# Moving residual passes, operand splits and gate rows in the instruction streams of VectorE and ScalarE of a two-layer transformer trunk

## The chip, the cores and the metric

The kernel runs on one core of a Trainium2 chip, as one launch. The metric is the device time of a run in microseconds. Of the kernel before there are three timed runs: 1076.07, 1076.11 and 1076.93 us, median 1076.11 us. One further execution was profiled; the rows below come from it.

## The reference

A trunk of two layers works on x (256 tokens, 1024 channels, float32). From a condition vector c come nine vectors of shift, scale and gate per layer, and two more for the shared keys and values. Each layer has three sub-layers, and each ends in a residual and a LayerNorm:

```python
def post_norm_residual(x, y, gate, weight, g, b):
    return layer_norm(DEEPNORM_ALPHA * x + weight * (1.0 + gate[:, None, :]) * y, g, b)
# cond = silu(c); per layer l:
mod = (cond @ w_ada[l] + b_ada[l]).reshape(b, 9, d)
h = modulate(x, mod[:, 0], mod[:, 1])                 # x * (1 + scale) + shift
x = post_norm_residual(x, swiglu(h, w_ffn_in[l, 0], w_ffn_out[l, 0]), mod[:, 2], 0.5, ...)
h = modulate(x, mod[:, 3], mod[:, 4])
# layer 0: q, k, v from h; rotary on 32 of 128 dims of q and k; causal softmax (256 tokens are one block)
# layer 1: q from h; k, v shared, from x before the layer; stick-breaking attention
y = merge_heads(y) @ w_o[l]
x = post_norm_residual(x, y, mod[:, 5], 1.0, ...)
h = modulate(x, mod[:, 6], mod[:, 7])
x = post_norm_residual(x, swiglu(h, w_ffn_in[l, 1], w_ffn_out[l, 1]), mod[:, 8], 0.5, ...)
```

There are 8 heads of 128 dims; the FFN has 2816 inner channels, done here in 11 steps of 256.

## The kernel before, in words

Every weight matrix is read once from HBM in 164 chunks of 128 x 2048 float32 (1 MB). SyncE loads chunk n into one of five buffers `raw`. ScalarE copies it to a float32r tile, the high part (`split_hi(n)`, L504); VectorE subtracts that from the raw chunk and gives the low part (`split_lo(n)`, L837). TensorE then makes each product of three float32r matmuls: high by high, low by high, high by low (`three`, L1253 to L1255 for products of the modulated input; `add_rows`, L1328 to L1330 for products that add up the sub-layer's output). High and low tiles have five places (`SPL`); a chunk may be split only when the chunk that held its place has been used. SyncE may load chunk n when chunk n-5 has its low part.

There is no scheduler and no planner: each engine has one stream of instructions, written out by hand, and runs it strictly in that order. Engines meet through semaphores alone. So an instruction that waits holds back all that stands behind it on its engine.

The stages in order are: FFN 0 (chunks 0 to 32), norm 0, QKV projection with rotary turn and softmax attention (33 to 44), output projection (45 to 48), norm 1, FFN 1 (49 to 81), norm 2, shared keys and values (82 to 89), FFN 2 (90 to 122), norm 3, Q projection and stick-breaking attention (123 to 126), output projection (127 to 130), norm 4, FFN 3 (131 to 163), last norm. `n` in a stage is its first chunk.

- An FFN step s on token tile t (two tiles of 128 tokens): TensorE `wide` (gate and up products), ScalarE `silu`, VectorE `inner` (L894, the product, tile `tmp`), TensorE transposes it (`turn_inner`, L1361), ScalarE keeps the high part (L512), VectorE the low part (`inner_lo`, L898), TensorE `add_rows`.
- A norm (`norm(i)`): VectorE `residual` (L980, L981) per half tile, mean (L986), ScalarE `deviation` (L593 square with sum, L596 root), VectorE `normalise` (L991, L994), TensorE transposes the result (`turn_normed`, L1275), and ScalarE and VectorE form the modulated input in high and low parts (`h_tile`). Here `lead` puts the first product of the next stage around the second tile's transposes.
- The residual stream itself, x = normed * g + b, is made later on VectorE by `x_scaled` (L1001) and `x_shifted` (L1006), 128 x 1024 each, one per tile. The queries' and keys' tiles share memory with the normed values, so ScalarE's `keep_heads` waits for `x_scaled`.
- Conditioning: each of the 20 vectors is a sum over 8 rows of 128 x 1024 (`ada`, 512 KB each), weighed by c. GpSimd issues the load of a row as soon as the row two before it was consumed, into two buffers; VectorE adds it (`accumulate(u, q)`, L869 or L861, two rows a call: a quarter). TensorE adds over the partitions (`turn_unit` L1288, or `spread_gate` L1296 for a gate).
- Attention of layer 0, per head: scores on TensorE, `soft_max` (VectorE, row maxima), `soft_exp` (ScalarE), `soft_scale` (VectorE, L1112 to L1114, the probabilities), `turn_probs` (TensorE, L1502), `keep_probT` (ScalarE, L665, L666), `weigh_values` (TensorE, L1440, L1441), `keep_yT` (high part ScalarE L611, low part VectorE L1056). `rope` (L1098 to L1101) turns queries and keys before `turn_tile` (L1424).
- Attention of layer 1, per head: `stick_scores` (TensorE, L1594, L1595), `stick_logs` (ScalarE, three passes), `stick_sums` (VectorE, L1224 to L1227), `stick_log_weights` (TensorE, L1605), `stick_weights` (ScalarE, L786), `weigh_values`, `keep_yT`.

## Time and profile before

| | before |
|---|---|
| timed runs, median (us) | 1076.11 |
| profiled execution, device time (us) | 1077.93 |
| its span, first to last instruction (us) | 1076.1 |
| TensorE matmul busy (us, share) | 1021.9 (95%) |
| VectorE busy | 776.7 (72%) |
| ScalarE busy | 522.4 (49%) |
| GpSimd busy | 85.7 (8%) |
| DMA | 265.61 MB, mean 247 GB/s |

Busy time is the union of the instructions' durations on an engine; matmuls overlap, so 0.39 us is what one of 512 columns takes and 0.23 us the distance from one's start to the next's. In a timeline row the first number is the start in us from the span's start, the second the duration of the row (of all its `x` instructions), and in square brackets stands how long the engine sat idle before it and what ended that. Such an idle time is shorter than what the wait costs, since the row before it would have overlapped with the next.

### The profile page before, as it was taken

The numbers are of one execution on the slowest core, as the hardware profiler recorded it, in microseconds if no ns is written. First come the engines' busy times: TensorE is split into PE (matmuls) and PEld (weight loads), VectorE is DVE, ScalarE is ACT, GpSimd is POOL, SyncE is SP. The second block draws the span as 40 slices with busy tenths as digits, with TensorE's granted clock in tenths as the row PEclk, the third lists the DMA queues.
The fourth block names the chain that finished last, engine by engine and source line by source line (L and its number), as shares of the span: only waits on it lengthen the run. The fifth ranks groups of instructions, "written<-read, shape, count | busy, mean of one in ns | idle before, by whom it ended". The sixth has DMA issues, their size and how long they took to land.

```text
span 1076.1 us, 12357 instructions
## 1 busy us (share of the span) xinstructions
PE 1021.9 (95%) x4708; PEld 827.7 (77%) x4708; DVE 776.7 (72%) x908; ACT 522.4 (49%) x852; POOL 85.7 (8%) x160
## 2 busy tenths in 40 slices
PE   3799999999999899999999999999999899999997
PEld 1587888877787677888878888888877777888885
DVE  7578777688775798777777587777877768445485
ACT  1545444446555734444466544444466755434342
POOL 0011111001000011111100011111100000000010
PEclk9899999999999999999999999999999999999999
DMA  9979898955774299889847399888946447555551
GB/s 360 353 260 332 298 322 277 355 198 163 268 250 142 78 316 339 302 300 321 310 184 234 122 309 337 309 296 318 328 164 218 150 147 252 177 196 167 187 194 39
DMA packets 147490, 265.61 MB, mean 247 GB/s; under 512 B 8424, under 2 KB 98920, under 8 KB 147432
## 3 DMA queue, kind: packets, MB, share of 16 engines
q1 hardware_dynamic: 124448, 182.87, 49.5%
q0 software_dynamic: 20928, 75.53, 19.9%
q10 hardware_dynamic: 2056, 6.42, 1.9%
q8 instruction: 37, 0.61, 0.2%
q14 instruction: 21, 0.17, 0.0%
HBM read 263.75 MB, written 1.05 MB: 246 GB/s over the span
## 4 chain that ended last, share of the span: by engine, by line
PE 66%; DVE 16%; DMA 7%; ACT 6%; issue 4%; DVEq 0%; SPq 0%; ACTq 0%
PE psum L1253 13%; PE psum L1255 13%; PE psum L1254 13%; PE psum L1328 7%; PE psum L1330 7%; PE psum L1329 7%; DMA ada<-in_w_ada 6%; DVE w_lo L837 5%; DVE acc L869 5%; ACT w_hi L504 2%; PE psum L1361 1%; PE psum L1288 1%; ACT psum L593 1%; PE psum L1275 1%; DVE qT L980 1%
## 5 line engine op out<-in xcount | busy, mean ns | idle before, releaser
L837 DVE TENSOR_TENSOR w_lo<-raw,w_hi 128x2048 fp32r<-128x2048 f32 x164 | 371.3, 2286 | 59.1 <-ACT w_hi L504 59.1
L1253 PE MATMUL psum<-w_hi,hT_hi 128*128 128x512 f32 x896 | 357.9, 399 | 8.4 <-DVE w_lo L837 8.1
L1255 PE MATMUL psum<-w_hi,hT_lo 128*128 128x512 f32 x896 | 351.0, 392 | 0.0
L1254 PE MATMUL psum<-w_lo,hT_hi 128*128 128x512 f32 x896 | 350.0, 391 | 0.0
L504 ACT ACTIVATE w_hi<-raw 128x2048 fp32r<-128x2048 f32 x164 | 310.4, 1915 | 0.4 <-PE psum L1330 0.4
L1253 PEld LDWEIGHTS psum<-w_hi,hT_hi 128*128 128x128 f32 x896 | 168.9, 189 | 46.2 <-DVE w_lo L837 7.7
L508 ACT ACTIVATE tmp<-psum 128x256 f32<-128x256 f32 x88 | 33.8, 384 | 348.0 <-PE psum L1255 348.0
L869 DVE SCALAR_TENSOR_TENSOR acc<-ada,cond,acc 128x1024 f32<-128x1024 f32 x128 | 164.1, 1282 | 51.8 <-DMA ada<-in_w_ada 41.5
L1255 PEld LDWEIGHTS psum<-w_hi,hT_lo 128*128 128x128 f32 x896 | 168.9, 188 | 36.5
L1254 PEld LDWEIGHTS psum<-w_lo,hT_hi 128*128 128x128 f32 x896 | 169.3, 189 | 33.0
L1328 PE MATMUL psum<-w_hi,a_hi 128*128 128x512 f32 x368 | 150.5, 409 | 0.8 <-ACT kT L666 0.8
L1330 PE MATMUL psum<-w_hi,a_lo 128*128 128x512 f32 x368 | 143.9, 391 | 0.0
L1329 PE MATMUL psum<-w_lo,a_hi 128*128 128x512 f32 x368 | 143.6, 390 | 0.0
L444 POOL DMA_DIRECT2D ada<-in_w_ada x128 | 68.3, 534 | 740.3 <-DVE acc L869 554.7
L894 DVE TENSOR_TENSOR tmp<-psum,tmp 128x256 f32<-128x256 f32 x88 | 37.2, 422 | 90.7 <-ACT tmp L508 90.6
L1330 PEld LDWEIGHTS psum<-w_hi,a_lo 128*128 128x128 f32 x368 | 69.1, 188 | 15.1
L1328 PEld LDWEIGHTS psum<-w_hi,a_hi 128*128 128x128 f32 x368 | 69.1, 188 | 14.4 <-ACT kT L666 1.0
L1329 PEld LDWEIGHTS psum<-w_lo,a_hi 128*128 128x128 f32 x368 | 69.4, 188 | 13.5 <-issue 1.0
L554 ACT ACTIVATE psum<-psum 128x128 f32<-128x128 f32 x104 | 27.2, 261 | 31.8 <-PE psum L1288 31.8
L512 ACT ACTIVATE a_hi<-psum 128x256 fp32r<-128x256 f32 x84 | 31.9, 380 | 13.6 <-PE psum L1361 13.5
L593 ACT ACTIVATE psum<-qT,nmean 128x1024 f32<-128x1024 f32 x12 | 13.4, 1120 | 49.1 <-DVE nmean L986 49.1
L1361 PEld LDWEIGHTS psum<-cst,tmp 128*128 128x128 f32 x176 | 23.9, 140 | 17.2 <-DVE tmp L894 5.5
(151 smaller groups left out, 727.5 us busy)
## 6 DMA issues: line engine op xcount, KB each, us to landing
raw<-in_w_ffn_in SPq DMA_DIRECT2D x176, 512.0 KB, 5.0
ada<-in_w_ada POOLq DMA_DIRECT2D x128, 512.0 KB, 5.4
raw<-in_w_ffn_out SPq DMA_DIRECT2D x88, 512.0 KB, 6.0
raw<-in_w_qkv_a SPq DMA_DIRECT2D x24, 512.0 KB, 5.1
raw<-in_w_o SPq DMA_DIRECT2D x16, 512.0 KB, 4.3
ada<-in_w_kv_ada POOLq DMA_DIRECT2D x16, 512.0 KB, 5.2
raw<-in_w_kv_b SPq DMA_DIRECT2D x16, 512.0 KB, 6.4
raw<-in_w_ada SPq DMA_DIRECT2D x4, 1024.0 KB, 14.2
```

What stands on the lines that cost most here:

```text
L444: pool.dma_start(ada[:, row % 2, :], ada_view(w)[:, row, j * D:(j + 1) * D])\
L504: nc.scalar.activation(hi_of(n), slot_of(n), ACT.Copy).then_inc(w_hi_ready, 1)
L837: nc.vector.tensor_tensor(lo_of(n), slot_of(n), hi_of(n).bitcast(F32), ALU.subtract)\
L869: nc.vector.scalar_tensor_tensor(out=sums, in0=src[:, r, :], scalar=factor, in1=base, op0=ALU.mult, op1=ALU.add).then_inc(acc_steps, 1)
L894: nc.vector.tensor_tensor(a_full[t], gu[t][:, 256:512], silu_t[t], ALU.mult).then_inc(a_ready, 1)
L1253: nc.tensor.matmul(dst, s_hi, m_hi, start=start, stop=False)
L1254: nc.tensor.matmul(dst, s_hi, m_lo, start=False, stop=False)
L1255: return nc.tensor.matmul(dst, s_lo, m_hi, start=False, stop=stop)
L1328: nc.tensor.matmul(dst, hi, m[0], start=first and j == 0, stop=False)
L1329: nc.tensor.matmul(dst, hi, m[1], start=False, stop=False)
L1330: end = nc.tensor.matmul(dst, lo, m[0], start=False, stop=last and j == 1)
L1361: last = nc.tensor.transpose(inner_bank(s, t)[:, j, :], a_full[t][:, j * P:(j + 1) * P], ident)
```

## The change

No instruction is added or removed and none changes its operands. The streams of VectorE and ScalarE are put in another order at these places (TensorE's at one):

- In `norm(i)`, ScalarE makes the high part of the next stage's third chunk (`ahead`) between the first tile's `h_tile` and the second tile's `deviation`; it stood behind the norm.
- Start of an FFN that follows an attention (1 and 3), VectorE: the two `x_scaled` move from ahead of `split_lo(n + 3)` to behind `inner_lo(f, 0, 0)`, and the two `x_shifted` from steps 0 and 1 to steps 2 and 3, behind `inner`.
- Last FFN step, VectorE: `inner` stands ahead of `split_lo`, and `inner_lo(f, s - 1, 1)` ahead of the gate's last quarter.
- QKV stage, VectorE: the first `rope` stands ahead of `split_lo(n + 2)`, the first `soft_scale` ahead of `split_lo(n + 9)`. TensorE turns the last two heads' probabilities ahead of two `weigh_values`, and ScalarE keeps them ahead of the last values tile. ScalarE splits chunk `N_WO[0] + 5` ahead of `keep_gate(1)`.
- Stick-breaking stage: VectorE's `x_shifted`, the gate's quarters and the output chunks' splits move as the diff shows, and ScalarE's splits with them; `load_ln_rows(4)` moves from ahead of the loop over the heads into it (h == 6).

```diff
@@ scalar: ffn, norm
             def ffn(f):
                 first_unit, n = FIRST_UNIT[f], N_FFN[f]
-                split_hi(n + 2)
+                if f in (0, 2):
+                    split_hi(n + 2)
...
+                deviation(i, 0)
+                h_tile(h, 0)
+                split_hi(ahead)
+                deviation(i, 1)
...
+                h_tile(h, 1)
@@ scalar: attention of layer 0
             split_hi(N_WO[0] + 2)
+            keep_probT(6)
+            keep_probT(7)
             keep_values(v1, 1, 1)
             keep_yT(0, 2)
             keep_yT(0, 3)
-            keep_probT(6)
-            keep_probT(7)
             split_hi(N_WO[0] + 3)
             keep_yT(0, 4)
             keep_yT(0, 5)
             split_hi(N_WO[0] + 4)
+            split_hi(N_WO[0] + 5)
             keep_gate(1)
...
-            split_hi(N_WO[0] + 5)
-            norm(1, ACT.Silu)
+            norm(1, ACT.Silu, N_FFN[1] + 2)
@@ scalar: stick-breaking stage
-            split_hi(n + 2)
             keep_tile(q0, 0)
             split_hi(n + 3)
             keep_tile(q0, 1)
+            split_hi(N_WO[1])
...
             keep_heads(q0, 1, qT, 0, SCALE)
-            split_hi(N_WO[1])
+            split_hi(N_WO[1] + 1)
...
             keep_heads(q1, 0, qT, 1, SCALE)
+            split_hi(N_WO[1] + 2)
             keep_tile(q1, 1)
-            load_ln_rows(4)
...
-                if h in (5, 7, HEADS + 1):
-                    split_hi(N_WO[1] + (h - 3) // 2)
-                if h == HEADS + 2:
-                    split_hi(N_WO[1] + 4)
+                if h == 6:
+                    load_ln_rows(4)
+                if h > HEADS:
+                    split_hi(N_WO[1] + h - 6)
@@ vector: ffn
                 split_lo(n + 2)
                 inner(f, 0, 0)
-                if norm_before is not None:
-                    x_scaled(norm_before, 0)
-                    x_scaled(norm_before, 1)
                 split_lo(n + 3)
                 inner(f, 0, 1)
                 inner_lo(f, 0, 0)
                 if norm_before is not None:
-                    x_shifted(norm_before, 0)
+                    x_scaled(norm_before, 0)
+                    x_scaled(norm_before, 1)
...
-                    if s == 1 and norm_before is not None:
-                        x_shifted(norm_before, 1)
                     inner(f, s, 0)
+                    if s in (2, 3) and norm_before is not None:
+                        x_shifted(norm_before, s - 2)
...
                 s = STEPS - 1
+                inner(f, s, 0)
                 split_lo(n + 3 * s + 2)
-                inner(f, s, 0)
+                inner_lo(f, s - 1, 1)
                 quarter(s, 0)
-                inner_lo(f, s - 1, 1)
                 inner_lo(f, s, 0)
@@ vector: attention of layer 0
+            rope(q0, 0)
             split_lo(n + 2)
-            rope(q0, 0)
...
             soft_max(0)
+            soft_scale(0)
             split_lo(n + 9)
-            soft_scale(0)
@@ vector: stick-breaking stage
             split_lo(n + 2)
+            accumulate(gate_unit, 0)
+            split_lo(n + 3)
             x_scaled(3, 0)
-            split_lo(n + 3)
             x_scaled(3, 1)
-            accumulate(gate_unit, 0)
-            x_shifted(3, 0)
-            accumulate(gate_unit, 1)
-            x_shifted(3, 1)
             split_lo(N_WO[1])
...
-                if h == 1 or h == 3:
-                    accumulate(gate_unit, 2 + h // 2)
+                if h < 2:
+                    x_shifted(3, h)
...
-                if h in (5, 7, HEADS + 1):
-                    split_lo(N_WO[1] + (h - 3) // 2)
-                if h == HEADS + 2:
-                    split_lo(N_WO[1] + 4)
-                if h == 6:
+                if h in (1, 3, 6):
+                    accumulate(gate_unit, (h + 1) // 2)
+                if h in (2, 5):
+                    split_lo(N_WO[1] + (h + 1) // 3)
+                if h > HEADS:
+                    split_lo(N_WO[1] + h - 6)
+                if h == 7:
                     coefficients(6)
@@ tensor: attention of layer 0
             project(v1, 1)
+            turn_probs(6)
+            turn_probs(7)
             for h in (2, 3):
                 weigh_values(0, h, qT[:, h, :], kT[:, h, 0:P])
-            turn_probs(6)
-            turn_probs(7)
```

VectorE's stream at the start of the QKV stage, before. `w_lo` is a chunk's low part, the four rows with `h_full` and `cst` are one rotary turn, `x_sb<-qT,g_row` is `x_scaled`:

```order
L1120 CAST masks<-cst 128x128 x3
L837 TENSOR_TENSOR w_lo<-raw,w_hi 128x2048
L1098 TENSOR_TENSOR tmp<-h_full,cst 128x128
L1099 TENSOR_TENSOR tmp<-h_full,cst 128x128
L1100 TENSOR_TENSOR h_full<-tmp 128x4x16
L1101 TENSOR_TENSOR h_full<-tmp 128x4x16
L1001 TENSOR_TENSOR x_sb<-qT,g_row 128x1024
```

The same place on VectorE with the change (its line numbers are one off):

```order
L1119 CAST masks<-cst 128x128 x3
L1097 TENSOR_TENSOR tmp<-h_full,cst 128x128
L1098 TENSOR_TENSOR tmp<-h_full,cst 128x128
L1099 TENSOR_TENSOR h_full<-tmp 128x4x16
L1100 TENSOR_TENSOR h_full<-tmp 128x4x16
L838 TENSOR_TENSOR w_lo<-raw,w_hi 128x2048
L1000 TENSOR_TENSOR x_sb<-qT,g_row 128x1024
```

The rotary turn now stands ahead of the chunk's low part.

VectorE's stream at the start of FFN 1, before. `tmp<-psum,tmp` is `inner`, `a_lo` is `inner_lo`, `x_sb<-x_sb,b_row` is `x_shifted`, `acc` is a gate's or a vector's quarter:

```order
L837 TENSOR_TENSOR w_lo<-raw,w_hi 128x2048
L894 TENSOR_TENSOR tmp<-psum,tmp 128x256
L1001 TENSOR_TENSOR x_sb<-qT,g_row 128x1024 x2
L837 TENSOR_TENSOR w_lo<-raw,w_hi 128x2048
L894 TENSOR_TENSOR tmp<-psum,tmp 128x256
L898 TENSOR_TENSOR a_lo<-psum,a_hi 128x2x128
L1006 TENSOR_TENSOR x_sb<-x_sb,b_row 128x1024
L861 TENSOR_SCALAR acc<-ada,cond 128x1024
L869 SCALAR_TENSOR_TENSOR acc<-ada,cond,acc 128x1024
L837 TENSOR_TENSOR w_lo<-raw,w_hi 128x2048 x2
L1006 TENSOR_TENSOR x_sb<-x_sb,b_row 128x1024
L894 TENSOR_TENSOR tmp<-psum,tmp 128x256
```

The same place on VectorE with the change:

```order
L838 TENSOR_TENSOR w_lo<-raw,w_hi 128x2048
L895 TENSOR_TENSOR tmp<-psum,tmp 128x256
L838 TENSOR_TENSOR w_lo<-raw,w_hi 128x2048
L895 TENSOR_TENSOR tmp<-psum,tmp 128x256
L899 TENSOR_TENSOR a_lo<-psum,a_hi 128x2x128
L1000 TENSOR_TENSOR x_sb<-qT,g_row 128x1024 x2
L862 TENSOR_SCALAR acc<-ada,cond 128x1024
L870 SCALAR_TENSOR_TENSOR acc<-ada,cond,acc 128x1024
L838 TENSOR_TENSOR w_lo<-raw,w_hi 128x2048 x2
L895 TENSOR_TENSOR tmp<-psum,tmp 128x256
```

Two scaling passes stand behind the second chunk's low part, and no shifting pass stands in this piece.

VectorE's stream in the stick-breaking stage, before, from the first output chunk on. The three rows with `gate` as destination are one head's `stick_sums`:

```order
L837 TENSOR_TENSOR w_lo<-raw,w_hi 128x2048
L1224 SCALAR_TENSOR_TENSOR gate<-psum,tmp 128x384
L1226 TENSOR_TENSOR gate<-gate,cst 128x128
L1227 TENSOR_TENSOR gate<-gate,cst 128x128
L1224 SCALAR_TENSOR_TENSOR gate<-psum,tmp 128x384
L1226 TENSOR_TENSOR gate<-gate,cst 128x128
L1227 TENSOR_TENSOR gate<-gate,cst 128x128
L869 SCALAR_TENSOR_TENSOR acc<-ada,cond,acc 128x1024 x2
```

The same place on VectorE with the change:

```order
L838 TENSOR_TENSOR w_lo<-raw,w_hi 128x2048
L1220 SCALAR_TENSOR_TENSOR gate<-psum,tmp 128x384
L1222 TENSOR_TENSOR gate<-gate,cst 128x128
L1223 TENSOR_TENSOR gate<-gate,cst 128x128
L1005 TENSOR_TENSOR x_sb<-x_sb,b_row 128x1024
L1220 SCALAR_TENSOR_TENSOR gate<-psum,tmp 128x384
L1222 TENSOR_TENSOR gate<-gate,cst 128x128
L1223 TENSOR_TENSOR gate<-gate,cst 128x128
L1005 TENSOR_TENSOR x_sb<-x_sb,b_row 128x1024
L870 SCALAR_TENSOR_TENSOR acc<-ada,cond,acc 128x1024 x2
```

The shifting passes and a quarter (before, both quarters 0 and 1 stood ahead of this piece) now stand among the heads' sums; the quarter at its end is quarter 1, and it was quarter 2.

## Rows read from the trace of the kernel before

**Rows 1.** The page: busy us (share of the span) per engine.

```profile
PE 1021.9 (95%) x4708; PEld 827.7 (77%) x4708; DVE 776.7 (72%) x908; ACT 522.4 (49%) x852; POOL 85.7 (8%) x160
```

**Rows 2.** Waits of PE: who waited for whom, us in total, times, longest.

```profile
PE psum L1253 <- DVE w_lo L837: 8.1, 5, 3.6
```

**Rows 3.** Timeline of PE, QKV stage: start, duration, instruction, [idle before <-releaser].

```profile
253.76 0.39 PE L1254 MATMUL psum<-w_lo,hT_hi 128*128 128x512 f32 x1
253.99 0.39 PE L1255 MATMUL psum<-w_hi,hT_lo 128*128 128x512 f32 x1
255.43 0.65 PE L1424 MATMUL psum<-cst,h_full 128*128 128x128 f32 x4 [1.05 <-DVE h_full L1101]
...
289.22 0.55 PE L1502 MATMUL psum<-cst,tmp 128*128 128x128 f32 x3 [2.41 <-DVE tmp L1114]
...
329.82 0.50 PE L1328 MATMUL psum<-w_hi,a_hi 128*128 128x512 f32 x1 [0.76 <-ACT kT L666]
```

**Rows 4.** Timeline of DVE, QKV stage, norm 1 and FFN 1.

```profile
252.28 2.29 DVE L837 TENSOR_TENSOR w_lo<-raw,w_hi 128x2048 fp32r<-128x2048 f32 x1 [1.46 <-ACT w_hi L504]
...
286.21 2.29 DVE L837 TENSOR_TENSOR w_lo<-raw,w_hi 128x2048 fp32r<-128x2048 f32 x1 [2.78 <-ACT w_hi L504]
...
346.38 2.29 DVE L837 TENSOR_TENSOR w_lo<-raw,w_hi 128x2048 fp32r<-128x2048 f32 x1 [2.80 <-ACT w_hi L504]
...
371.76 2.35 DVE L1001 TENSOR_TENSOR x_sb<-qT,g_row 128x1024 f32<-128x1024 f32 x2
374.02 2.29 DVE L837 TENSOR_TENSOR w_lo<-raw,w_hi 128x2048 fp32r<-128x2048 f32 x1
```

**Rows 5.** Timeline of PE, from norm 1 to the KV stage.

```profile
351.88 0.39 PE L1330 MATMUL psum<-w_hi,hT_lo 128*128 128x512 f32 x1
354.16 1.11 PE L1275 MATMUL psum<-cst,qT 128*128 128x128 f32 x8 [1.89 <-DVE qT L994]
...
376.37 0.50 PE L1253 MATMUL psum<-w_hi,hT_hi 128*128 128x512 f32 x1 [1.26 <-DVE w_lo L837]
...
386.19 0.41 PE L1361 MATMUL psum<-cst,tmp 128*128 128x128 f32 x2 [1.09 <-DVE tmp L894]
...
407.06 1.06 PE L1288 MATMUL psum<-cst,acc 128*128 128x128 f32 x8 [0.81 <-DVE a_lo L898]
...
570.45 0.47 PE L1253 MATMUL psum<-w_hi,hT_hi 128*128 128x512 f32 x1 [0.34 <-DVE w_lo L837]
```

**Rows 6.** Timeline of PE, stick-breaking stage and start of FFN 3.

```profile
829.71 0.70 PE L1605 MATMUL psum<-gate,cst 128*128 128x256 f32 x2 [2.63 <-DVE gate L1227]
...
842.50 0.67 PE L1440 MATMUL psum<-tmp,v_sb 128*128 128x256 f32 x2 [3.44 <-DVE a_lo L1056]
...
895.45 0.50 PE L1253 MATMUL psum<-w_hi,hT_hi 128*128 128x512 f32 x1 [1.28 <-DVE w_lo L837]
```

**Rows 7.** Windows of the stick-breaking stage: length, busy per engine, clock, DMA share, GB/s.

```profile
826.40:855.10 28.70, 21.79 (x123) 18.45 (x124) 22.46 (x43) 19.12 (x37) 1.06 (x2) 0.94 0.51 176
...
830.70:834.10 3.40, 3.40 (x16) 2.98 (x14) 2.14 (x2) 2.52 (x5) 0.53 (x1) 0.50 0.97 326
```

**Rows 8.** Timeline of DVE, stick-breaking stage: quarters of the gate's sum.

```profile
822.64 2.67 DVE L869 SCALAR_TENSOR_TENSOR acc<-ada,cond,acc 128x1024 f32<-128x1024 f32 x2 [2.75 <-DMA ada<-in_w_ada]
...
839.33 2.68 DVE L869 SCALAR_TENSOR_TENSOR acc<-ada,cond,acc 128x1024 f32<-128x1024 f32 x2 [2.95 <-DMA ada<-in_w_ada]
```

**Rows 9.** Tile `ada` from 800 to 850 us: its transfers, issue to landing.

```profile
DMA to landing us min/median/max: 3.6/4.9/7.5
```

**Rows 10.** Timeline of PE, end of FFN 0.

```profile
221.50 0.44 PE L1361 MATMUL psum<-cst,tmp 128*128 128x128 f32 x2 [1.34 <-DVE tmp L894]
...
227.97 0.44 PE L1361 MATMUL psum<-cst,tmp 128*128 128x128 f32 x2 [0.17 <-DVE tmp L894]
```

**Rows 11.** Timeline of ACT in norm 1, around the second tile's square.

```profile
357.84 0.83 ACT L581 ACTIVATE hT_hi<-h_full 128x256 fp32r<-128x256 f32 x2
361.13 1.12 ACT L593 ACTIVATE psum<-qT,nmean 128x1024 f32<-128x1024 f32 x1 [2.47 <-DVE nmean L986]
```

25 lines of the change are left out of this document (10 added, 15 removed).

## Prediction

> **What bounds the kernel now.** I read the busy times of the engines first [rows 1]: TensorE has matmuls under way for 1021.9 of 1076.1 us, VectorE is busy 72%, ScalarE 49%. The change takes nothing from any engine, so it can only win idle time of TensorE, which is 1076.1 - 1021.9 = 54.2 us at most. Then the waits of TensorE by pairs [rows 2]: the largest one inside the stages is for low parts of weight chunks, 8.1 us in five places. The timeline of TensorE says where they are. The thirteen single waits at the seams between stages and in the attentions, 0.17 to 3.44 us each, sum to 18.5 us [rows 3, 5, 6, 10]. The others lie in the first 60 us, where inputs are awaited, and behind the last matmul, and nothing moves there. Inside the FFNs TensorE starts a 512-column matmul every 0.23 us (253.76 to 253.99, [rows 3]) and nothing can be won there. So each edit is worth the wait that it ends, less the wait that comes next in line. The price of a wait is read from starts and not from the idle column: 255.43 - 253.99 - 0.23 = 1.21 us where the column says 1.05 [rows 3], because the following matmul can't overlap.
>
> **First rotary turn, QKV stage.** The turn stood behind a low part that itself waited 1.46 us for ScalarE and ended at 252.28 + 2.29 = 254.57; TensorE went on 0.86 us later [rows 3, 4]. With the turn first (0.9 us of work; its input is there while VectorE still waits) it is done near 251.8, while TensorE is free at 254.2. The low part behind it no longer waits, since its high part is made in the norm (`ahead`); it ends at about 254.1, just as TensorE asks for it, and the next at 257.4, 0.2 us before it is needed. Gain 1.2 us; bounds 0.6 and 1.2.
>
> **First probabilities.** The scaling stood behind a low part that waited 2.78 us and ended at 288.50; TensorE waited 2.41 us for it, 2.6 with the restart [rows 3, 4]. Scaled first, the probabilities are ready at 285.1, before TensorE asks (286.6). What is late next: that low part still starts at 286.2, so head 1's maxima start at 289.3 where they started at 290.6, 1.3 us earlier against TensorE's 2.6, and by head 2's turn TensorE waits 0.3 us. Gain 2.3 us; bounds 1.3 and 2.6.
>
> **Last probabilities.** TensorE began the output product at 329.82 after 0.76 us for ScalarE's copies [rows 3]. With turns and copies first, two `weigh_values` (1.3 us) cover the copies (1.0 us). Gain 0.9 us; bounds 0.5 and 1.0.
>
> **Norm 1.** TensorE stood from 351.88 + 0.23 to 354.16, 2.05 us, for the normalised tile [rows 5]. The cause is at 346.38: VectorE sat idle 2.80 us until ScalarE, busy with the gate and a table load, had made the high part of one more chunk, and its 2.29 us low part stands ahead of the residual [rows 4]. With that high part made before the gate, VectorE does the low part in its idle time and starts the residual at 345.7 instead of 348.6. Then TensorE's own second half tile (348.0) sets the chain. The other norms, where nothing else is late, lose 0.3 us at this place. Gain 1.75 us; bounds 1.5 and 2.0.
>
> **Starts of FFN 1 and 3.** In FFN 1 the low part of 374.02 stands behind two scaling passes of 2.35 us [rows 4], and TensorE waits for it 1.26 us, then 1.09 us for `inner` behind a shifting pass, then 0.81 us for an `inner_lo` [rows 5]. Without the passes and 1.38 us earlier at the first low part, the first is done at 372.6, before TensorE needs it at 375; `inner` of step 1 at 382.4, against 383.6. Both waits go: 1.42 + 1.26 = 2.7 us. But TensorE then reaches the third place 2.7 us earlier, and VectorE, who still has two scaling passes and now a shifting pass ahead of it, is there only 2 to 2.7 us earlier, depending on how fast the rows of the conditioning sum land. So I count 2.4, with bounds 1.6 and 2.9. FFN 3 has no sums there; its one wait of 1.28 us [rows 6] goes whole: 1.4, bounds 1.2 and 1.4.
>
> **KV stage.** 0.34 us for a low part that `ahead` brings forward [rows 5]: 0.5 with the restart, bounds 0.3 and 0.5.
>
> **End of FFN 0.** TensorE waits 1.34 us for `inner`, which now comes 2.2 us earlier. I count nothing. VectorE does the same list of work from 216.6 to 230 without a gap; it still delivers the gate's sum at 224.3, and the `inner` after which TensorE waits at 227.97 was late by 0.17 us already [rows 10]. TensorE arrives 1.3 us earlier and waits that time there. Bounds 0 and 0.4. In FFN 1 and 2 the gate's sum comes 0.33 us later than it did, which is about the room it has: bounds -0.2 and 0 each.
>
> **Stick-breaking stage.** From 826.4 to 855.1 TensorE is busy 21.79 of 28.70 us, and 3.40 us of this run at half clock [rows 7], so at full clock it has 21.79 - 1.70 = 20.1 us of work, and at most 8.6 us can be won. Two waits hold most of it [rows 6]. The first, 2.63 us until 829.71, is for head 0's sums, whose input lay ready while VectorE waited 2.75 us for rows of the gate [rows 8] and did a shifting pass and a low part. The second, 3.44 us until 842.50, is for a low part behind a quarter that waited 2.95 us for its rows [rows 8]. Now quarter 0 comes right after norm 3 (its rows, asked for at 803 to 804, land in the meantime by any of the times of [rows 9]), quarter 1's rows land during the projection, and heads 0 and 1 are summed by 824.4, before TensorE wants them at 826.9. The first wait goes. Quarter 2's rows can be asked for only at 826.9 and 828.2, when quarter 1 is done; they land between 833 and 835.7 by the extremes of 4.9 and 7.5 us [rows 9]. Behind quarter 2 stand head 4's sums, behind an output chunk's low part head 6's, and behind quarter 3 the spread gate. Going through the heads by their durations, TensorE waits 1.0 us at head 4, 0.65 at head 6 and 1.85 for the gate's sum (done at 844.8), and 0.3 in restarts: 3.8 us are left of 8.6. Gain 4.8 us; bounds 3.4 (rows at 7.5 us) and 8.3 (nothing left but the restarts).
>
> The clock is part of that sum. Its granted rate was 0.50, the 1.2 GHz level, from 830.7 to 834.1, after TensorE had stood for 2.63 us; the longer stand until 842.50 brought no fall [rows 6, 7]. By the Trainium skill ("TensorE: Matmul & The Clock Gate", "Part 1: The HAM clock gate") the gate follows how busy the array has been, on a clock that runs free of the kernel. The one fall and the one that stayed out agree with this.
>
> The Trainium skill ("DMA: Bandwidth & Descriptors", "Anatomy of one DMA") gives a transfer from GpSimd's queue as 2.0 us plus bytes over 436 GB/s, an estimate of 3.2 us for a row of 512 KB. The trace has 4.9 at the median here [rows 9]. By 3.2 us quarter 2 would wait for nothing and the term would be about 5.3.
>
> **The sum.** 1.2 + 2.3 + 0.9 + 1.75 + 2.4 + 1.4 + 0.5 + 0 + 4.8 = 15.25 us. Off the span of 1076.1 it leaves 1060.9. The profiled execution took 1077.93 us with 1.8 us around its span; the median of the timed runs is 1076.11, 1.8 less. I predict for timed runs: 1076.1 - 15.2 = 1060.9 us.
>
> **Rivals.**
> A new bound behind the old one: VectorE has no slack where the waits go, and TensorE meets it again a few us later. For it: the end of FFN 0 does just that, and rows take up to 7.5 us. Against it: at most seams VectorE itself was idle for ScalarE (1.46, 2.78, 2.80 us, [rows 4]). With the lower bounds of all terms: 0.6 + 1.3 + 0.5 + 1.5 + 1.6 + 1.2 + 0.3 - 0.4 + 3.4 = 10.0, so 1066.1 us.
> All waits gone, VectorE always in time: the upper bounds, 1.2 + 2.6 + 1.0 + 2.0 + 2.9 + 1.4 + 0.5 + 0.4 + 8.3 = 20.3, so 1055.8 us. Against it: quarters 2 and 3 can't come earlier than their rows.
> The clock falls elsewhere: the waits left at heads 4, 6 and the gate come within 8 us, and a fall of 3.4 us as the one seen costs 1.7 us: 1062.6. By the rule named above this can happen; the 3.44 us stand without a fall speaks against it.
> Slower: `split_hi(ahead)` stands in ScalarE's stream ahead of the second tile's square, on which normalise, transposes and the next stage's first product hang. ScalarE has a gap there of 2.47 us and the split takes 1.9 [rows 11], which leaves 0.5. If the chunk or its place is not ready, all of the delay goes to TensorE, in each of five norms. It decides from a delay of 15.2 / 5 = 3.0 us beyond the 0.5; at 3.5 us the time is 1076.1 - 15.2 + 17.5 = 1078.4. Against it: the place is freed by the first of the three last chunks, about 2.2 us before ScalarE comes, and the raw chunk landed long ago.
> No change (all won is waited for elsewhere, 1076): only if TensorE weren't the bound; [rows 1] speak against.
>
> **Chances.** Forecast 0.58, new bound 0.20, clock 0.07, all gone 0.09, slower 0.03, no change 0.03. The range reaches to the new bound's time and most of the way to the other end: 1057 to 1067. A measurement can tell 0.2% (2.2 us) from no change; faster 0.94, same 0.03, slower 0.03.
>
> **What would show it.** Right: the waits at the first rotary turn, first probabilities, norm 1 (down to 0.3 us) and FFN 3 gone; the half-clock stretch gone; output product of layer 1 starting 4.8 us sooner against the end of norm 3; at FFN 0's end the 1.34 us moved to the gate's spread or to the next `inner`. Wrong: a wait of TensorE for the second tile's transposes in the norms over 0.3 us, or DMA named as releaser of ScalarE's splits.

## The result and the profile after

The changed kernel took 1058.91 us (median of 4 runs, 1057.72 to 1061.44) against 1076.15 us (1076.07 to 1076.93) for the one before in the same comparison: ratio 0.9841, 95% interval 0.9826 to 0.9856. Forecast were 1060.9 us and a range of 1057 to 1067. The profiled execution took 1057.72 us, its span is 1055.9 us.

The page after, busy us per engine. It answers to [rows 1]: the same instructions kept TensorE busy for 4.8 us less; one stretch at half clock fewer is part of that.

```profile
PE 1017.1 (96%) x4708; PEld 826.3 (78%) x4708; DVE 775.5 (73%) x908; ACT 521.4 (49%) x852; POOL 85.7 (8%) x160
```

Waits of TensorE after: us in total, times, longest. They answer to [rows 2].

```profile
PE psum L1251 <- DVE w_lo L838: 4.1, 2, 3.6
PE psum L1286 <- DVE acc L870: 3.1, 1, 3.1
PE psum L1294 <- DVE acc L870: 2.8, 5, 1.8
PE psum L1286 <- DVE tmp L870: 1.9, 1, 1.9
PE psum L1286 <- DVE a_lo L899: 1.8, 2, 1.3
PE psum L1603 <- DVE gate L1223: 1.1, 2, 0.6
```

The low parts of weight chunks are late in two places instead of five; both lie in the first 50 us, where inputs are awaited. What is left inside the stages is the gate's spread (L1294, five times), one wait ahead of the first sums' transposes in FFN 1 (L1286 for `a_lo`; the other one, of 0.5 us, is in FFN 0, where the kernel before had 1.00 us) and two heads (L1603).

Timeline of TensorE after, at the places of [rows 3, 5]: the first rotary turn, the first probabilities, the output product, the second half of norm 1, and FFN 1's sums.

```profile
249.39 0.39 PE L1253 MATMUL psum<-w_hi,hT_lo 128*128 128x512 f32 x1
249.62 0.60 PE L1422 MATMUL psum<-cst,h_full 128*128 128x128 f32 x4
...
280.57 0.49 PE L1500 MATMUL psum<-cst,tmp 128*128 128x128 f32 x3
...
320.43 0.48 PE L1326 MATMUL psum<-w_hi,a_hi 128*128 128x512 f32 x1
...
342.93 1.11 PE L1273 MATMUL psum<-cst,qT 128*128 128x128 f32 x8
...
393.02 1.06 PE L1286 MATMUL psum<-cst,acc 128*128 128x128 f32 x8 [1.28 <-DVE a_lo L899]
```

Four places where TensorE had stood for 1.05, 2.41, 0.76 and 1.89 us have no brackets any more: the turn follows the matmul before it after 0.23 us. Only the last row still waits, and longer than the 0.81 us of [rows 5].

To compare the two span by span I read the starts of the first transposes of each norm. Distances in us, with a second profile of each kernel (columns "again"):

| from, to | before | before again | after | after again | forecast gain |
|---|---|---|---|---|---|
| start, FFN 0's first sums | 90.00 | 86.84 | 86.57 | 86.35 | 0 |
| to norm 0 | 146.74 | 144.77 | 145.58 | 145.52 | 0 |
| QKV to norm 1 | 117.42 | 118.98 | 110.78 | 110.79 | 6.15 |
| FFN 1 to norm 2 | 198.32 | 197.22 | 195.71 | 196.92 | 2.4 |
| KV, FFN 2 to norm 3 | 241.87 | 242.24 | 241.65 | 241.69 | 0.5 |
| stick-breaking to norm 4 | 78.90 | 79.48 | 74.20 | 72.80 | 4.8 |
| FFN 3 to the end | 202.85 | 202.97 | 201.41 | 201.43 | 1.4 |

The 20.2 us between the first two spans are not all the change's: 3.4 us lie in the first row, where nothing moved. The first profile of before has 10.2 us at half clock there and after 6.8, which makes an estimated 1.7 us; the rest are longer waits for the same instructions. What lies behind the first row, 16.8 us, agrees with the 17.2 us between the timed medians.

### The profile page after: what moved, and what is told of

The parts are those of the page before. It is cut to its first block, busy times and chain, and to the rows that moved or that the text cites. A ratio compares the mean times of both kernels' runs of the same rounds, so it can differ in the third digit from the quotient of the medians.

```text
span 1055.9 us, 12357 instructions
## 1 busy us (share of the span) xinstructions
PE 1017.1 (96%) x4708; PEld 826.3 (78%) x4708; DVE 775.5 (73%) x908; ACT 521.4 (49%) x852; POOL 85.7 (8%) x160
## 3 DMA queue, kind: packets, MB, share of 16 engines
HBM read 263.75 MB, written 1.05 MB: 251 GB/s over the span
## 4 chain that ended last, share of the span: by engine, by line
PE 70%; DVE 17%; DMA 5%; ACT 4%; issue 3%; DVEq 0%; SPq 0%; ACTq 0%
PE psum L1251 14%; PE psum L1253 14%; PE psum L1252 14%; PE psum L1328 7%; PE psum L1326 7%; PE psum L1327 7%; DVE w_lo L838 5%; DVE acc L870 5%; DMA ada<-in_w_ada 4%; PE psum L1359 1%; PE psum L1286 1%; ACT psum L594 1%; ACT w_hi L504 1%; PE psum L1273 1%; DVE qT L980 1%
## 5 line engine op out<-in xcount | busy, mean ns | idle before, releaser
L512 ACT ACTIVATE a_hi<-psum 128x256 fp32r<-128x256 f32 x84 | 31.9, 380 | 10.2 <-PE psum L1359 10.2
L899 DVE TENSOR_TENSOR a_lo<-psum,a_hi 128x256 fp32r<-128x256 f32 x84 | 34.9, 415 | 0.0
```

Of the source, the lines that this page charges most:

```text
L899: nc.vector.tensor_tensor(inner_part(s, t, 1), inner_bank(s, t), inner_part(s, t, 0).bitcast(F32), ALU.subtract).then_inc(a_lo_ready, 1)
```

## Experiments

Times are medians of timed runs, in us, ratios to the kernel before with a 95% interval.

**The two kernels again.**

> The kernel before, unchanged. In the two profiles so far the first transposes of FFN 0's sums (unit 2) start at 90.0 us before and 86.6 us after, though no instruction up to there was moved; half-clock stretches at 45.7 to 52.5 us stand in the one and not in the other. Theory A (the start's clock varies from run to run and 3.4 of the 20.2 us between the two spans are not the change's): this run shows another start, with the transposes anywhere from 86 to 91 us, and from there on the same distances as the first profile within 0.3 us, FFN 0's end apart. Rival (the start is fixed for a kernel): 90.0 us again, and the 3.4 us belong to the change in a way not seen.

> The changed kernel, unchanged. Its four timed runs spread over 3.7 us (1057.7 to 1061.4) where the kernel before spread over 0.9. Theory A: the spread is the start's clock and the half-clock stretch in the stick-breaking stage, so a profile of another run has its norms at 110.8, 306.5 and 548.1 us' distance as before (from norm 0's first transposes at 232.2: 342.9, 538.6, 780.3) within 0.5 us, and differs ahead of the first and perhaps behind 822 us. Rival: the distances between norms themselves vary by 1 us or more, as row landings do.

Before: 1074.45 (1072.54 to 1077.62), ratio 0.999 [0.9973, 1.0007]. After: 1058.86 (1057.3 to 1059.92), 0.9832 [0.9807, 0.9857]. In both, theory A is right about the start (86.84 and 86.35 us) and wrong about the rest: the second profile of before differs by up to 1.6 us in a stage, and FFN 1 took 1.2 us longer in after's second. The distances between norms vary too, as the second rival had it. The second profile of before shows what a wait can cost beyond itself. Its windows (length, busy per engine, clock, DMA share, GB/s) and its TensorE timeline at the first probabilities:

```profile
285.40:288.80 3.40, 3.40 (x10) 2.62 (x10) 1.51 (x6) 2.45 (x5) 0.00 (x0) 0.50 0.61 235
```

```profile
284.08 0.55 PE L1502 MATMUL psum<-cst,tmp 128*128 128x128 f32 x3 [2.42 <-DVE tmp L1114]
...
285.70 0.63 PE L1254 MATMUL psum<-w_lo,hT_hi 128*128 128x512 f32 x1
286.12 0.63 PE L1255 MATMUL psum<-w_hi,hT_lo 128*128 128x512 f32 x1
```

After the 2.42 us stand the granted clock is 0.50 for 3.4 us, the 1.2 GHz level, and a matmul follows the last after 0.42 us, not 0.23. Such a stretch costs 1.7 us where TensorE has work throughout, and less where it would have waited anyway: the stick-breaking stage of before again has 10.2 us at half clock, that of before 3.4, and it took only 0.6 us longer. The first profile has the same wait without it [rows 3]; with the change wait and stretch are both gone. So the QKV stage won 6.6 us against the first profile and 8.2 against the second.

Span times mean granted clock gives an estimate of a run without its stretches. For the 19 timed runs of before beside these two it is 1064.6 us (mean span 1073.8, mean clock 0.9914), for the four of after 1050.3 us (1057.0, 0.9938). By this estimate 14.3 of 16.8 us are waits and 2.5 are clock; the forecast had 15.25 - 1.7 = 13.55 and 1.7. It is a rough one: it counts stretches in which TensorE waited in full, and the ten runs of before again, the same kernel, give 1061.8 us.

**The end of FFN 0.** Only the order of the last FFN step on VectorE, in the kernel before:

```diff
                 s = STEPS - 1
+                inner(f, s, 0)
                 split_lo(n + 3 * s + 2)
-                inner(f, s, 0)
+                inner_lo(f, s - 1, 1)
                 quarter(s, 0)
-                inner_lo(f, s - 1, 1)
                 inner_lo(f, s, 0)
```

> The kernel before with only the last FFN step's order changed on VectorE. The prediction counted nothing for it: the 1.34 us wait for inner in FFN 0 moves to the gate's spread or the next inner; span within 0.4 us of before, start aside. The comparison of the two profiles shows 1.2 us less from FFN 0's first sums (unit 2) to norm 0. Theory A: that 1.2 us came from rows of the gate that landed earlier (VectorE waited 3.6 us for them in the profile before and 1.8 us in the changed kernel's), so it is there or not there with the landings, and the span's gain is 0 to 0.4 us. Rival B: the new order itself is worth 1.2 us in FFN 0, and nothing in the other FFNs.

Measured 1076.29 (1073.09 to 1080.2), 1.0002 [0.9983, 1.0021]. The stage took 145.58 us, as in after; before's two profiles have 146.74 and 144.77. TensorE:

```profile
220.33 1.96 PE L1296 MATMUL psum<-acc,neg_ones 128*128 128x512 f32 x4 [0.27 <-DVE acc L869]
```

In the timed runs the edit is worth nothing. The wait for `inner` is gone and a short one for the gate's spread stands there. But before again has no wait for `inner` at this place either, with the old order, and was faster still; so whether the first profile's 1.34 us are there at all varies from run to run, which is in line with theory A; rival B is out.

**The remaining waits of the stick-breaking stage.** After, timeline of TensorE, and the window behind the last of these waits:

```profile
822.24 0.70 PE L1603 MATMUL psum<-gate,cst 128*128 128x256 f32 x2 [0.60 <-DVE gate L1223]
...
827.09 0.70 PE L1603 MATMUL psum<-gate,cst 128*128 128x256 f32 x2 [0.54 <-DVE gate L1223]
...
830.11 3.39 PE L1294 MATMUL psum<-acc,neg_ones 128*128 128x512 f32 x4 [1.76 <-DVE acc L870]
```

```profile
829.60:833.00 3.40, 2.89 (x4) 1.37 (x5) 2.24 (x9) 0.00 (x0) 0.00 (x0) 0.50 0.75 262
```

By starts they cost 0.81, 0.74 and 1.91 us; the forecast was 1.0, 0.65 and 1.85. First edit: the spread gate behind the last head. Second: besides, VectorE adds the last quarter at h == 7, behind that head's sums, not at h == 6.

```diff
@@ late_spread, tensor
-                if h == HEADS:
-                    pe.wait_ge(head_kept, 16)
-                    spread_gate(4)
...
+            pe.wait_ge(head_kept, 16)
+            spread_gate(4)
             output_rows(1, 0)
@@ heads_first, vector, besides
-                if h in (1, 3, 6):
-                    accumulate(gate_unit, (h + 1) // 2)
+                if h in (1, 3, 7):
+                    accumulate(gate_unit, {1: 1, 3: 2, 7: 3}[h])
```

> The changed kernel with TensorE's spread of the stick-breaking stage's gate moved from head 8's turn to behind the last head. In the changed kernel TensorE waits 1.76 us for the gate's sum there (1.9 with the restart) and runs the spread at half clock, 3.39 us instead of 1.9. Theory A (the wait is for the sum alone, and the clock fell because of it): the wait goes, the spread takes 1.9 us, no half-clock stretch in this stage, 3.4 us faster in all (span 1052.5 with the same start). Rival B (the clock falls in this stage for its many short matmuls, whatever the waits): the wait goes, 1.9 us, but a 3.4 us stretch at half clock stays and costs up to 1.7 us: 1.9 us faster. Rival C (VectorE is the bound of the stage's end): head 7's sums are late instead and little is won, under 0.8 us.

> The changed kernel with the spread of the stick-breaking gate behind the last head (as in the run before this one) and, new, VectorE's third quarter of its sum behind head 7's stick_sums where it stood behind head 6's. With the spread alone moved, TensorE's wait went from the spread to head 7's log weights (1.96 us), since the quarter's 2.67 us stand ahead of head 7's sums. Theory A (VectorE's work in this order is the bound of the stage's end): head 7's wait goes, the spread's stays under 0.5 us; norm 3's first transposes to norm 4's take 71.0 us where the changed kernel has 72.8 (without a half-clock stretch) and 74.2 (with one); no half-clock stretch. Rival (the landings of the quarter's rows set it): the quarter is just as late as before and TensorE waits 1 to 2 us at the spread: 72.8.

Measured 1062.05 (1058.66 to 1062.74), 0.9856 [0.9828, 0.9884], and 1060.62 (1058.04 to 1061.95), 0.9861 [0.9845, 0.9878]. TensorE in the one and in the other:

```profile
836.07 0.70 PE L1603 MATMUL psum<-gate,cst 128*128 128x256 f32 x2 [1.96 <-DVE gate L1223]
```

```profile
838.23 0.67 PE L1438 MATMUL psum<-tmp,v_sb 128*128 128x256 f32 x2 [1.70 <-DVE hT_lo L1055]
```

The wait of 1.76 us moved to the last head's sums, and then to the product of values whose bank VectorE had still to read. Norm 3 to norm 4 took 73.07 and 72.66 us, against 72.80 in after again: nothing won. That is rival C of the first expectation; of the second the rival has the time (72.66 us, 72.8 expected) but not the place, since TensorE no longer waits at the spread. In both places what stands behind the quarter (2.7 us) was late. Both were slower in FFN 1, where the instructions are after's (200.18 and 199.10 us against 195.71). TensorE and the clock there, in late_spread:

```profile
395.52 0.87 PE L1286 MATMUL psum<-cst,acc 128*128 128x128 f32 x3 [2.95 <-DVE a_lo L899]
```

```profile
398.10:401.50 3.40, 3.40 (x9) 2.64 (x8) 3.30 (x3) 3.40 (x14) 1.05 (x2) 0.50 0.94 292
```

**The wait in FFN 1.** After, timeline of VectorE ahead of it:

```profile
376.42 0.41 DVE L899 TENSOR_TENSOR a_lo<-psum,a_hi 128x256 fp32r<-128x256 f32 x1
378.59 2.67 DVE L870 SCALAR_TENSOR_TENSOR acc<-ada,cond,acc 128x1024 f32<-128x1024 f32 x2 [1.76 <-DMA ada<-in_w_kv_ada]
...
385.92 1.21 DVE L1005 TENSOR_TENSOR x_sb<-x_sb,b_row 128x1024 f32<-128x1024 f32 x1
387.06 2.66 DVE L870 SCALAR_TENSOR_TENSOR acc<-ada,cond,acc 128x1024 f32<-128x1024 f32 x2
389.64 0.42 DVE L899 TENSOR_TENSOR a_lo<-psum,a_hi 128x256 fp32r<-128x256 f32 x1
```

VectorE stands 1.76 us for rows, a shifting pass follows, and the `a_lo` on which TensorE waits is late. The edit moves the passes on, one to a step, into steps 3, 5 and 7:

```diff
                 inner_lo(f, 0, 0)
-                if norm_before is not None:
-                    x_scaled(norm_before, 0)
-                    x_scaled(norm_before, 1)
...
-                    if s in (2, 3) and norm_before is not None:
-                        x_shifted(norm_before, s - 2)
+                    if s in (3, 5) and norm_before is not None:
+                        x_scaled(norm_before, s // 2 - 1)
+                    if s == 7 and norm_before is not None:
+                        x_shifted(norm_before, 0)
+                        x_shifted(norm_before, 1)
```

> The changed kernel with FFN 1's and 3's residual passes moved on: x_scaled into steps 3 and 5, both x_shifted into step 7. In FFN 1 TensorE waited for inner_lo(2, 0) ahead of the transposes of the first sums: 0.8 us in the kernel before, 1.3, 2.6 and 3.0 us in three profiles of the changed order, and in the last of these a half-clock stretch of 6.8 us followed. VectorE has 2.3 + 1.1 us of passes ahead of that point. Theory A (VectorE's work up to that point is the bound): 3.4 us less ahead of it, the wait is gone or under 0.5 us, no half-clock stretch there, and norm 1's first transposes to norm 2's take 194 to 194.7 us (195.7 to 200.2 in the three). Rival B (the rows' landings are the bound: VectorE waits longer for them by what it saves): the wait stays over 1 us and the stretch takes over 195.5 us.

Measured 1056.90 (1056.42 to 1058.1), 0.9831 [0.9817, 0.9846], the lowest median of all, though its interval overlaps that of after. TensorE, then VectorE:

```profile
394.48 1.03 PE L1286 MATMUL psum<-cst,acc 128*128 128x128 f32 x8
```

```profile
380.28 2.68 DVE L870 SCALAR_TENSOR_TENSOR acc<-ada,cond,acc 128x1024 f32<-128x1024 f32 x2 [2.10 <-DMA ada<-in_w_kv_ada]
```

VectorE still waits for rows (2.10 us), but TensorE waits no more; norm 1 to norm 2 is 194.21 us, and 194.22 in the one other kernel with this edit. Theory A holds. The opposite edit puts the passes back where they were before the change:

```diff
                 inner(f, 0, 0)
+                if norm_before is not None:
+                    x_scaled(norm_before, 0)
+                    x_scaled(norm_before, 1)
                 split_lo(n + 3)
                 inner(f, 0, 1)
                 inner_lo(f, 0, 0)
                 if norm_before is not None:
-                    x_scaled(norm_before, 0)
-                    x_scaled(norm_before, 1)
+                    x_shifted(norm_before, 0)
...
                     split_lo(n + 3 * s + 2)
+                    if s == 1 and norm_before is not None:
+                        x_shifted(norm_before, 1)
                     inner(f, s, 0)
-                    if s in (2, 3) and norm_before is not None:
-                        x_shifted(norm_before, s - 2)
```

> The changed kernel with the scaling and shifting passes of the residual in FFN 1 and 3 back where they were before the change. Prediction's step: the low part of the second chunk (1.26 us) and inner (1.09 us) are late again in FFN 1 and 1.28 us come back in FFN 3; less what the later place loses. First transposes of norm 1 to those of norm 2 about 197.5 us against 195.7 (196.9 in a second profile of after), norm 4 to the end 202.8 against 201.4: 1058.9 + 1.5 + 1.4 = 1061.8 us (1060.5 to 1063). Rival (in FFN 1 the wait is only carried to the first sums' transposes, 1.3 to 3.2 us there in the four profiles with the change, so the passes' move is worth nothing there, and FFN 3 alone counts): norm 1 to norm 2 195.7 to 196.9, time 1060.3.

Measured 1058.24 (1056.12 to 1061.74), 0.9837 [0.9811, 0.9862], below both expectations and no different from after. TensorE in FFN 1:

```profile
374.45 0.41 PE L1361 MATMUL psum<-cst,tmp 128*128 128x128 f32 x2 [1.10 <-DVE tmp L895]
...
394.90 1.06 PE L1288 MATMUL psum<-cst,acc 128*128 128x128 f32 x8 [0.45 <-DVE a_lo L899]
```

The 1.26 us wait for the low part in [rows 5] doesn't come back, though both passes stand ahead of it again; `ahead` alone had ended it. The other two sum to 1.55 us, where after's one was 1.28 and 2.56 us in its two profiles. FFN 1 took 196.64 us, between after's two profiles, FFN 3 201.86, 0.45 us more than after.

**The high part made ahead.** First it goes behind the norm, which is its old place in FFN 1, FFN 3 and the Q stage (in the QKV and the KV stage the kernel before had it one copy later still); then two chunks' high parts stand ahead of the second tile's square:

```diff
@@ ahead_behind
                 h_tile(h, 0)
-                split_hi(ahead)
                 deviation(i, 1)
...
                 h_tile(h, 1)
+                split_hi(ahead)
@@ two_ahead (and the later split_hi of the same chunk left out)
                 split_hi(ahead)
+                split_hi(ahead + 1)
                 deviation(i, 1)
```

> The changed kernel with split_hi(ahead) behind the norm again, in all five norms, everything else as changed. Theory A (the split ahead of the second tile's square costs nothing and is worth the first low part of the next stage 1.4 us earlier): 0.3 to 0.6 us lost in the QKV stage, 0.5 at the KV stage, 0 to 0.3 in FFN 3, 0.5 to 1.4 in FFN 1, together 1.5 to 3 us slower than the changed kernel. Rival (the split in the norm delays the square a little in each norm): norm 1's second transposes come sooner than 9.37 us behind the first, and the whole is no slower.

> The changed kernel with two chunks' high parts instead of one between the first tile's h_tile and the second tile's deviation on ScalarE, in all five norms. This tries the mechanism of the slower rival. ScalarE's gap there is 2.47 us; two splits take 3.7 us. Theory (ScalarE's work ahead of the square goes to TensorE as soon as it is over the gap): the second transposes come 9.38 + 1.3 = 10.7 us behind the first in each norm, TensorE waits 1.3 us more there, five times: 5 to 6.5 us slower than the changed kernel, still faster than before. Rival (the next stage's low parts, now 1.9 us earlier still, give it back): under 2 us slower.

Measured 1065.12 (1063.84 to 1065.79), 0.9905 [0.9888, 0.9921], and 1064.23 (1062.32 to 1066.31), 0.9898 [0.9882, 0.9915]. Without `ahead` TensorE waits at the starts of the QKV and the Q stage, and in FFN 1:

```profile
250.47 0.47 PE L1251 MATMUL psum<-w_hi,hT_hi 128*128 128x512 f32 x1 [0.69 <-DVE w_lo L838]
253.71 0.50 PE L1251 MATMUL psum<-w_hi,hT_hi 128*128 128x512 f32 x1 [0.26 <-DVE w_lo L838]
...
397.40 1.94 PE L1286 MATMUL psum<-cst,acc 128*128 128x128 f32 x8 [3.66 <-DVE a_lo L899]
...
809.39 0.50 PE L1251 MATMUL psum<-w_hi,hT_hi 128*128 128x512 f32 x1 [0.81 <-DVE w_lo L838]
```

This is 6.2 us slower than the changed kernel, twice the 3 us of theory A's upper end. The QKV stage took 112.23 us (110.78 in after), FFN 1 201.75, FFN 3 201.84. Most of the excess is FFN 1, with its wait of 3.66 us and 6.8 us at half clock; kernels that keep `ahead` have waits of up to 3.39 us there too, so how much of it is `ahead`'s was not separated. The KV stage has no wait at its start, though the high part is not made in the norm: there it was enough to make it ahead of ScalarE's copy. And the waits at the starts of the QKV and the Q stage are not waits of the kernel before: they come from the new order, which puts other work ahead of a low part there and needs `ahead` to pay for it.

With two high parts, the waits of TensorE by pairs, and ScalarE in norm 1, then ScalarE there in after:

```profile
PE psum L1272 <- DVE qT L992: 5.5, 5, 1.1
```

```profile
350.76 3.70 ACT L504 ACTIVATE w_hi<-raw 128x2048 fp32r<-128x2048 f32 x2
354.37 1.09 ACT L595 ACTIVATE psum<-qT,nmean 128x1024 f32<-128x1024 f32 x1
```

```profile
349.89 1.12 ACT L594 ACTIVATE psum<-qT,nmean 128x1024 f32<-128x1024 f32 x1 [0.66 <-DVE nmean L985]
```

ScalarE's gap of [rows 11] holds one split of 1.9 us, not two: the square starts late, and in each of the five norms the second transposes stand 10.40 us behind the first, not 9.38. 5 x 1.02 = 5.1 us of the 5.4 us between this median and after's, as the theory had it. The mechanism of the slower rival is real; one split stays inside the gap, with 0.66 us to spare.

**The first low parts in the QKV stage.** The changed kernel with the two vector edits of that stage undone:

```diff
+            split_lo(n + 2)
             rope(q0, 0)
-            split_lo(n + 2)
...
+            split_lo(n + 9)
             soft_scale(0)
-            split_lo(n + 9)
```

> The changed kernel with the first rope behind split_lo(n + 2) and the first soft_scale behind split_lo(n + 9), as before the change; the third chunk's high part is still made in the norm. Theory (the rotary turn was late only because the low part ahead of it waited 1.46 us for its high part; with that made in the norm, low part and turn are both done by about 254.0 us while TensorE is free at 254.2, so the rope's move is worth nothing beside ahead; the chunk of soft_scale still waits for ScalarE): no wait at the first rotary turn, 2.2 us back at the first probabilities, from the gate's spread in FFN 0's end to norm 1 113.0 us against 110.8, time 1061.1 (1060.3 to 1062). Rival (each move is worth what the prediction gave it, 1.2 and 2.3 us): 114.3 us, time 1062.4.

Measured 1063.28 (1060.18 to 1064.72), 0.9882 [0.9861, 0.9904]. TensorE:

```profile
251.71 0.60 PE L1422 MATMUL psum<-cst,h_full 128*128 128x128 f32 x4
...
285.24 0.55 PE L1500 MATMUL psum<-cst,tmp 128*128 128x128 f32 x3 [2.42 <-DVE tmp L1113]
...
399.55 1.09 PE L1286 MATMUL psum<-cst,acc 128*128 128x128 f32 x8 [3.39 <-DVE a_lo L899]
```

No wait at the rotary turn: its move is worth nothing beside `ahead`. The probabilities' wait is back whole; norm 0 to norm 1 took 113.11 us, 2.33 more. That is the theory's number; the time is over its range. In the profile the rest lies ahead of FFN 0's sums, where nothing moved, and in FFN 1 (199.91 us), where the wait was 3.39 us and half clock followed at 400.5 us, as in late_spread.

**The stick-breaking stage in its old order** (VectorE and ScalarE; `ahead` kept; the edit is that part of the change's diff reversed).

> The changed kernel with the stick-breaking stage in the order of before on VectorE and ScalarE; norm 3 still makes the third chunk's high part ahead. Theory (the stage's gain is its own, 4.8 us forecast, 4.7 and 6.1 in two profiles with and without a stretch at half clock): norm 3 to norm 4 78.5 to 79.4 us, time 1058.9 + 5.5 = 1064.4 (1063 to 1065.5). Rival (the gain comes in part from norm 3's ahead, which starts the stage's first low part earlier): 76 to 77.5 us, time 1061.5 to 1063.

Measured 1065.13 (1060.95 to 1067.82), 0.9896 [0.9872, 0.9919]. TensorE, and the clock behind the last row:

```profile
815.97 0.70 PE L1603 MATMUL psum<-gate,cst 128*128 128x256 f32 x2 [1.50 <-DVE gate L1225]
...
827.66 1.07 PE L1438 MATMUL psum<-tmp,v_sb 128*128 128x256 f32 x2 [3.49 <-DVE a_lo L1054]
```

```profile
827.80:831.20 3.40, 3.40 (x11) 2.87 (x12) 2.29 (x8) 2.01 (x2) 0.00 (x0) 0.50 0.02 5
```

The stage took 77.14 us against before's 78.90, both with one stretch at half clock: 1.8 us of its gain are `ahead`'s, 1.1 of them at head 0, whose wait shrank from 2.63 to 1.50 us. (The edit also puts ScalarE's table load back ahead of `keep_gate(4)`; the change has it behind, which the list of the change leaves out.) The expectation's two measures disagree: the profile (77.14) speaks for the rival, the median for the theory (1064.4). The changed kernel took 74.20 us with a stretch, so the order itself is worth 2.9 us in this stage. By span times clock the six runs have 1053.4 us at a mean clock of 0.9912, after 1050.3 at 0.9938: by this rough estimate 3.1 us of the 5.8 between the mean spans are waits and the rest clock.

**Both remaining waits out of the way.** passes_odd with the gate's last quarter at h == 8, behind head 5's low part, and its spread inside the output projection, as layer 0 has it.

```diff
-                if h == HEADS:
-                    pe.wait_ge(head_kept, 16)
-                    spread_gate(4)
...
             output_rows(1, 1, (0,))
+            spread_gate(4)
             output_end(1)
@@ vector
-                if h in (1, 3, 6):
-                    accumulate(gate_unit, (h + 1) // 2)
+                if h in (1, 3, 8):
+                    accumulate(gate_unit, {1: 1, 3: 2, 8: 3}[h])
...
-                if h == 7:
+                if h == 8:
                     coefficients(6)
```

> The kernel passes_odd with the gate's last quarter moved behind the attention of layer 1: VectorE adds it at h == 8, behind the low part of head 5, and TensorE spreads the gate inside the output projection, behind output_rows(1, 1, (0,)), as in layer 0. Theory (TensorE waited 1.9 us for the spread only because the quarter stood ahead of it in time, and VectorE has 7 us idle between 831 and 849 us to do it in): the spread's wait goes and nothing replaces it, the waits of 0.8 and 0.7 us at heads 4 and 6 stay; second transposes of norm 3 to those of norm 4 72.8 - 1.9 = 70.9 us, time 1056.9 - 1.9 = 1055.0 us (1054 to 1056). Rival (VectorE bound from head to head, as heads_first showed: each place taken by a quarter is late for what stands behind it): the low parts of heads 6 and 7 or the chunks of the output projection are late instead, 72.3 to 73 us, time 1056.5 to 1057.

Measured 1057.02 (1056.63 to 1059.53), 0.983 [0.9808, 0.9852]: nothing beside passes_odd. Norm 3 to norm 4 took 74.92 us by the second transposes, more than either side had. The theory was wrong; the rival has the time and names the output projection's chunks, but not why one was late. ScalarE, VectorE and TensorE in the output projection and norm 4:

```profile
839.72 1.03 ACT L568 ACTIVATE gate<-psum 128x1024 f32<-128x1024 f32 x1 [6.44 <-PE psum L1294]
840.76 1.28 ACT L819 ACT_TABLE_LOAD   x1
842.06 1.92 ACT L504 ACTIVATE w_hi<-raw 128x2048 fp32r<-128x2048 f32 x1
```

```profile
844.01 2.29 DVE L838 TENSOR_TENSOR w_lo<-raw,w_hi 128x2048 fp32r<-128x2048 f32 x1 [7.50 <-ACT w_hi L504]
846.22 0.68 DVE L979 TENSOR_TENSOR qT<-psum,gate 128x512 f32<-128x512 f32 x1
```

```profile
851.78 1.39 PE L1273 MATMUL psum<-cst,qT 128*128 128x128 f32 x8 [2.53 <-DVE qT L993]
```

The heads were free of the quarter (no wait for the spread, none for a value bank). But `split_hi(N_WO[1] + 5)` stands behind `keep_gate(4)` on ScalarE, and so does the table load of 1.28 us, which the change had moved there; the gate came at 839.7 us after ScalarE had idled 6.44 us. VectorE idled 7.50 us for that chunk, and the residual behind it began 67.7 us after norm 3's first transposes (846.22 - 778.48), in passes_odd 66.0 us after. All that TensorE had won by then became a stand of 2.53 us in norm 4, with half clock behind it (852.5 to 855.9 us). This is the norm 1 pattern of [rows 4], which the change itself cured in layer 0 by putting that split ahead of the gate. The same edit here was not tried.

## Why the prediction was right, step by step

- **TensorE's idle time is the budget.** Right: 14.3 us of waits came out by the estimate above, 13.55 forecast. Two readings were off without weight in the sum: of the 8.1 us for low parts in [rows 2] only 2.9 are inside the stages, and the list of single waits leaves out 1.00 us at 90.0 us, which is no start-up wait, and 0.54 at 848.98.
- **First rotary turn, probabilities, last probabilities, norm 1.** 6.15 us forecast together, 6.64 measured (117.42 to 110.78). The feared 0.3 us at head 2 did not come. The 2.3 us of the probabilities are shown (2.33). The rotary turn's gain is there, but `ahead` alone brings it, not the move. The other two were not tested apart. Against the two other profiles with the old order here (118.98 and 119.06 us, each with a stretch at half clock behind the probabilities) the gain is 8.2 and 8.3 us.
- **FFN 1.** Forecast 2.4; 2.6 in the first pair of profiles. That agreement is luck: over six profiles of kernels with this order from norm 1 to norm 2 (after twice, late_spread, heads_first, stick_undone, chunk_first) it took 195.7 to 200.2 us, mean 197.9, where before's two took 198.3 and 197.2. On average the stage won nothing. The step that failed is "VectorE is there only 2 to 2.7 us earlier". Counted from norm 1, the third place began 50.1 to 52.2 us on, mean 51.3, where the three profiles with the old order have 51.9 to 52.9, mean 52.2: 0.9 us earlier. VectorE came sooner and waited longer for rows (1.8 to 3.9 us, against 0.7 to 1.9), TensorE waited 1.3 to 3.4 us there, where [rows 5] had 0.81, and three times the clock fell, which took the rest. The bounds of 1.6 and 2.9 were too narrow below.
- **FFN 3.** 1.44 us, forecast 1.4. Putting back either half alone costs about 0.45 us (201.86 without the moved passes, 201.84 without `ahead`, one profile each): the same wait was covered twice.
- **KV.** The wait of 0.34 us is gone. Net 0.2 us, forecast 0.5; kernels with this order lie between 241.4 and 242.8 us, so the profiles can't tell.
- **End of FFN 0.** Nothing in the timed runs, as forecast. The mechanism is shown in part: the wait for `inner` gave way to one at the gate's spread, but of 0.24 to 0.27 us, not of the 1.3 us named.
- **Stick-breaking stage.** The three waits left were sized right (3.5 us with restarts, 3.8 forecast). Forecast 4.8; measured 4.7 with a stretch at half clock and 6.1 without, against the first profile of before. "Half-clock stretch gone" was true of some executions only: it followed the spread's 1.76 us in one profile of after and not in the other. 1.8 us of the gain belong to `ahead`.
- **Rivals.** A new bound behind the old one is what FFN 1 and both late-gate kernels show, but locally. The clock did fall elsewhere, and yet cost less in sum: there are fewer long waits for it to follow. The slower rival needs more than one split.

The forecast was 2.0 us too high against the first comparison. Other sets of runs of the kernel before have medians of 1074.45 to 1075.92 us, so the gain is 15.6 to 17.2 us, and the excess over the forecast 0.4 to 2.0. That the sum came out so close is in part luck: FFN 1 gave on average nothing of its 2.4 us, and over all profiles with the old and the new order the QKV stage gave 7.7 us and the stick-breaking stage 5.8, together 2.6 more than forecast, in part because there are fewer stretches at half clock.

## What to carry to other kernels

Where a low-priority instruction stands ahead of the one the bottleneck wants, first ask what the low-priority one waits for: making its input earlier (one high part, inside a gap of 2.47 us that it fits) ended or cut the waits at the starts of four stages (QKV, FFN 1, stick-breaking, FFN 3), and the moves of the rotary turn and, in FFN 1, of the passes then bought nothing beside it. After taking a wait out, read the next place where the same two engines meet, with the slowest landing of its transfers. And before an instruction is moved later, list what stands behind its reader on each engine: here a split that had nothing to do with the gate stood behind it on ScalarE, and the residual behind the split.

## What the runs showed of the hardware

The granted clock fell to 0.50 behind single waits of TensorE of 1.76 to 3.66 us, but not behind each: 2.56 us ahead of FFN 1's sums in after again, 1.76 us at the spread in passes_odd and 3.44 us in before [rows 6] had no stretch behind them. Some falls came within the wait and not behind it (829.6 us in after, where the wait ended at 830.11). A stretch lasted 3.4 us, or 6.8 us as in ahead_behind, late_spread and before again. So a wait of about 2 us or more costs its length, and now and then 1.7 us or more on top where TensorE has work throughout. By the Trainium skill ("TensorE: Matmul & The Clock Gate", "Part 1: The HAM clock gate") the gate samples on its own clock, not the kernel's; equal waits with and without a fall, as here, agree. This accounts for part of the spread between runs of one kernel: passes_undone has spans of 1054.3 us at a mean clock of 0.997 and 1059.9 at 0.991.
